# Weight buffers with slack, each weight piece at its own one of sixteen starts 32 bytes apart

## The reference

```python
# block 1 (retention and latent attention)
h = x @ w_in                         # 1024 -> 7744
o = retention(...), causal_attention(rms_norm(mq) @ w_uq, rms_norm(mkv) @ w_ukv)
x = layer_norm(DN_ALPHA * x + concat(gated o) @ w_out)      # 3072 -> 1024
# block 2 (16 heads of attention, gated)
h = x @ w_in                         # 1024 -> 4096
x = layer_norm(DN_ALPHA * x + (merge(o) * silu(g)) @ w_out) # 1024 -> 1024
# block 3 (band attention with 8 heads, a state space mixer, then the feed-forward part)
h = rmsnorm(x) @ w_in_2              # 1024 -> 4112
x = x + concat(attention, ssd) @ w_out_2                    # 1536 -> 1024
x = x + relu(rmsnorm(x) @ w_ff1_2) ** 2 @ w_ff2_2           # 1024 -> 4096 -> 1024
out = rmsnorm(x)
```

## Time and profile before

| | before |
|---|---|
| runs, us | 795.87, 791.13 (median 793.5) |
| profiled execution, span, us | 790.2 |
| its own time | between the runs and the span nothing more is listed; the span is 0.9 us under the faster run |
| PE busy, share of the span | 775.5 us, 98% |
| weight loads (PEld) | 680.4 us, 86% |
| VectorE, ScalarE, GpSimd busy | 65%, 52%, 12% |
| DMA, share of 16 engines' span, hardware and software queue | 52.1%, 1.8% |
| granted TensorE clock | 0.999 of full speed (2.4 GHz) |

### The profile page before, as it was taken

One profiled execution on the slowest core, in us unless ns is written; L12 is line 12 of the kernel. 1 busy time (PEld: TensorE's weight loads), 2 busy tenths in 40 slices (PEclk: granted clock), 3 DMA queues, 4 the chain that ended last, 5 costly groups with the idle time before them and its releaser, 6 DMA issues.

```text
span 790.2 us, 13096 instructions
## 1 busy us (share of the span) xinstructions
PE 775.5 (98%) x5084; PEld 680.4 (86%) x5084; DVE 512.6 (65%) x816; ACT 414.6 (52%) x623; POOL 95.4 (12%) x69
## 2 busy tenths in 40 slices
PE   9999999999999999999999899999999999999997
PEld 8998877799978887999787799889777999999996
DVE  6965656666664658468866874877756755555554
ACT  5534445453664453445765667465655544445443
POOL 2332000000100003111400207500000000000002
PEclk9999999999999999999999999999999999999999
DMA  9855653344664644676832564634217576556541
GB/s 337 320 182 191 203 171 106 120 150 123 200 229 160 185 150 145 209 227 185 260 88 98 164 199 130 206 110 158 86 65 223 188 220 208 176 197 203 174 157 53
DMA packets 77051, 137.43 MB, mean 174 GB/s; under 512 B 7104, under 2 KB 15552, under 8 KB 76992
## 3 DMA queue, kind: packets, MB, share of 16 engines
q1 hardware_dynamic: 75744, 132.15, 52.1%
q0 software_dynamic: 1248, 4.46, 1.8%
HBM read 132.80 MB, written 1.05 MB: 169 GB/s over the span
## 4 chain that ended last, share of the span: by engine, by line
PE 90%; DVE 4%; issue 2%; POOL 2%; ACT 1%; POOLq 0%; ACTq 0%; DVEq 0%
PE acc L1051 13%; PE acc L1053 13%; PE acc L1052 13%; PE acc L1059 13%; PE acc L1061 12%; PE acc L1060 12%; PE acc L1339 1%; PE acc L1373 1%; DVE w_lo L780 1%; PE acc L1216 1%; PE acc L1323 1%; PE acc L1312 1%; PE acc L1252 1%; PE acc L1208 1%; POOL b_lo L780 1%
## 5 line engine op out<-in xcount | busy, mean ns | idle before, releaser
L780 DVE TENSOR_TENSOR w_lo<-raw,w_hi 128x1024 fp32r<-128x1024 f32 (+1 forms) x224 | 273.5, 1236 | 174.0 <-ACT w_hi L760 91.9
L1059 PE MATMUL acc<-x_hi,w_hi 128*128 128x256 f32 x840 | 236.7, 282 | 0.4 <-DVE x_lo L2201 0.4
L1061 PE MATMUL acc<-x_hi,w_lo 128*128 128x256 f32 x840 | 233.9, 278 | 0.0
L1060 PE MATMUL acc<-x_lo,w_hi 128*128 128x256 f32 x840 | 233.9, 278 | 0.0
L760 ACT ACTIVATE w_hi<-raw 128x1024 fp32r<-128x1024 f32 (+1 forms) x128 | 133.3, 1043 | 131.8 <-PE acc L1061 66.4
L750 ACT ACTIVATE w_hi<-raw 128x1024 fp32r<-128x1024 f32 x109 | 115.9, 1063 | 110.9 <-PE acc L1061 58.6
L1059 PEld LDWEIGHTS acc<-x_hi,w_hi 128*128 128x128 f32 x840 | 157.9, 188 | 3.4 <-issue 2.6
L1060 PEld LDWEIGHTS acc<-x_lo,w_hi 128*128 128x128 f32 x840 | 158.6, 189 | 0.8 <-issue 0.5
L1061 PEld LDWEIGHTS acc<-x_hi,w_lo 128*128 128x128 f32 x840 | 158.2, 188 | 0.0
L1051 PE MATMUL acc<-w_hi,cat_hi 128*128 128x512 f32 x272 | 108.9, 400 | 0.2 <-DVE w_lo L780 0.2
L1053 PE MATMUL acc<-w_hi,cat_lo 128*128 128x512 f32 x272 | 107.0, 393 | 0.0
(11 more groups left out here) (297 smaller groups left out, 910.1 us busy)
## 6 DMA issues: line engine op xcount, KB each, us to landing
raw<-in_w_ff SPq DMA_DIRECT2D x32, 1024.0 KB, 5.3
raw<-in_w_in_even SPq DMA_DIRECT2D x28, 1024.0 KB, 5.0
raw<-in_w_in_odd SPq DMA_DIRECT2D x16, 1024.0 KB, 5.4
raw<-in_w_in SPq DMA_DIRECT2D x16, 1024.0 KB, 5.6
raw<-in_w_out_even SPq DMA_DIRECT2D x12, 1024.0 KB, 5.1
raw<-in_w_out SPq DMA_DIRECT2D x4, 1024.0 KB, 5.0
raw<-in_w_in_even SPq DMA_DIRECT2D x4, 512.0 KB, 6.6
raw<-in_w_ukv_even SPq DMA_DIRECT2D x8, 256.0 KB, 3.2
```

What stands on the lines that cost most here:

```text
L780: ins = eng.tensor_tensor(lo, r, hi.bitcast(F32), ALU.subtract)
L1059: pe.matmul(o, wh[:, k, fs], hi[:, ka, :], start=start and f % 2 == 0, stop=False, skip_group_check=True)
L1060: pe.matmul(o, wh[:, k, fs], lo[:, ka, :], start=False, stop=False, skip_group_check=True)
L1061: ins = pe.matmul(o, wl[:, k, fs], hi[:, ka, :], start=False, stop=stop, skip_group_check=True)
```

## The change

Three things change. The descriptor ring is 8192 bytes. `w_hi` and `w_lo` get 128 floats (512 bytes) of slack behind each half, so each is 18432 bytes and not 16384. And each piece gets a `shift` of 8 * (i // 2 * 5 % 16) floats, where i counts the pieces of its layout: places 0, 160, 320, 480, 128 ... bytes, sixteen of them, multiples of 32 bytes, the same for two pieces in a row. The 192 bytes of gap that stood ahead of `x_hi` now stand ahead of `w_hi`. Worked out as above: `w_hi` starts at 36864, `w_lo` at 55296, `x_hi` at 81920, `b_hi` at 98304, `v_hi` at 131072, `cat_hi` at 175104, all multiples of 512. So the distance of a matmul is now the shift of its piece, and 0 still for `v` and `b`. The list of instructions of every engine stays the same, in the same order, with the same waits; only addresses differ. Counted over the program:

| distance, bytes | 0 | 32 | 64 | 96 | 128 | 160 | 192 | 224 | 256 | 288 | 320 | 352 | 384 | 416 | 448 | 480 |
|---|---|---|---|---|---|---|---|---|---|---|---|---|---|---|---|---|
| 256-column matmuls after, feat and tok | 240 | 96 | 192 | 216 | 192 | 192 | 96 | 192 | 144 | 192 | 192 | 96 | 192 | 144 | 192 | 216 |
| 512-column matmuls after | 192 | 96 | 66 | 72 | 48 | 144 | 96 | 66 | 72 | 96 | 120 | 48 | 96 | 84 | 96 | 108 |

Before, 48 of the 512-column and 48 of the 256-column ones are at distance 0 and all others at 320.

```diff
+SLACK = 128
...
-        w_hi = sb("w_hi", [P, 2, 2048], F32R)
-        w_lo = sb("w_lo", [P, 2, 2048], F32R)
+        sb("w_gap", [P, 48])
+        w_hi = sb("w_hi", [P, 2, 2 * (HALF + SLACK)], F32R)
+        w_lo = sb("w_lo", [P, 2, 2 * (HALF + SLACK)], F32R)
         res = sb("res", [P, T, D])
-        sb("x_gap", [P, 48])
...
+        for layout, apart in (("feat", 2), ("tok", 2)):
+            for i, p in enumerate(q for q in pieces if q.chunk.layout == layout):
+                p.shift = 8 * (i // apart * 5 % 16)
...
+        def place(p, e):
+
+            if p.home in (0, 1):
+                return p.off + e + (p.off + e) // HALF * SLACK + p.shift
+            return p.off + e
+
+        def weights_of(p):
+
+            def tiles(b):
+                return [b[:, place(p, k * p.cols):place(p, k * p.cols) + p.cols] for k in range(p.nk)]
+            return [tiles(b) for b in room_of(p)]
+
         def split_views(p, k0, k1):
...
-            parts = [b[:, p.off + k0 * p.cols:p.off + k1 * p.cols] for b in room_of(p)]
+            at = place(p, k0 * p.cols)
+            parts = [b[:, at:at + (k1 - k0) * p.cols] for b in room_of(p)]
...
-                wh, wl = [b[:, p.off:p.off + p.size].rearrange("p (k n) -> p k n", k=p.nk) for b in room_of(p)]
+                wh, wl = weights_of(p)
...
-                            pe.matmul(o, xh, wh[:, k, :], start=start, stop=False)
+                            pe.matmul(o, xh, wh[k], start=start, stop=False)
...
-    nc = _bacc.Bacc("TRN2", target_bir_lowering=False, num_devices=1)
+    nc = _bacc.Bacc("TRN2", target_bir_lowering=False, num_devices=1, dynamic_dma_scratch_size=8192)
```

More of the change, by code:

```diff
@@ L125, in __init__ @@
         self.off = 0
+        self.shift = 0
         self.home = None
@@ L686, in split_views @@
             if p.order == "beside":
-                both = room_of(p)[0][:, p.off:p.off + 2 * p.size].rearrange("p (k c n) -> p k c n", k=p.nk, c=2)
+                both = room_of(p)[0][:, at:at + 2 * p.size].rearrange("p (k c n) -> p k c n", k=p.nk, c=2)
                 return [(r.rearrange("p (k n) -> p k n", k=p.nk), both[:, :, 0, :], both[:, :, 1, :])]
@@ L1050, in products_of @@
                             xh, xl = hi[:, ka, t * P:(t + 1) * P], lo[:, ka, t * P:(t + 1) * P]
-                            pe.matmul(o, xh, wh[:, k, :], start=start, stop=False)
-                            pe.matmul(o, xh, wl[:, k, :], start=False, stop=False)
-                            ins = pe.matmul(o, xl, wh[:, k, :], start=False, stop=stop or (t == 1 and k == p.nk - 1 and p is down[1].pieces[-2]))
+                            pe.matmul(o, xh, wh[k], start=start, stop=False)
+                            pe.matmul(o, xh, wl[k], start=False, stop=False)
+                            ins = pe.matmul(o, xl, wh[k], start=False, stop=stop or (t == 1 and k == p.nk - 1 and p is down[1].pieces[-2]))
                     else:
@@ L1057, in products_of @@
                             fs = slice(f * P, (f + 1) * P)
-                            pe.matmul(o, wh[:, k, fs], hi[:, ka, :], start=start and f % 2 == 0, stop=False, skip_group_check=True)
-                            pe.matmul(o, wh[:, k, fs], lo[:, ka, :], start=False, stop=False, skip_group_check=True)
-                            ins = pe.matmul(o, wl[:, k, fs], hi[:, ka, :], start=False, stop=stop, skip_group_check=True)
+                            pe.matmul(o, wh[k][:, fs], hi[:, ka, :], start=start and f % 2 == 0, stop=False, skip_group_check=True)
+                            pe.matmul(o, wh[k][:, fs], lo[:, ka, :], start=False, stop=False, skip_group_check=True)
+                            ins = pe.matmul(o, wl[k][:, fs], hi[:, ka, :], start=False, stop=stop, skip_group_check=True)
                     if p.full and k == p.nk // 2 - 1:
@@ L1082, in products_of_tokens @@
                     xh, xl = hi[:, ka, t * P:(t + 1) * P], lo[:, ka, t * P:(t + 1) * P]
-                    pe.matmul(o, xh, wh[:, k, :], start=start, stop=False)
-                    pe.matmul(o, xh, wl[:, k, :], start=False, stop=False)
-                    ins = pe.matmul(o, xl, wh[:, k, :], start=False, stop=stop)
+                    pe.matmul(o, xh, wh[k], start=start, stop=False)
+                    pe.matmul(o, xh, wl[k], start=False, stop=False)
+                    ins = pe.matmul(o, xl, wh[k], start=False, stop=stop)
                     if t and k == 1:
@@ L1102, in last_columns @@
                     xh, xl = hi[:, ka, P:2 * P], lo[:, ka, P:2 * P]
-                    pe.matmul(o, xh, wh[:, k, cs], start=k == 0, stop=False)
-                    pe.matmul(o, xh, wl[:, k, cs], start=False, stop=False)
-                    ins = pe.matmul(o, xl, wh[:, k, cs], start=False, stop=k == p.nk - 1)
+                    pe.matmul(o, xh, wh[k][:, cs], start=k == 0, stop=False)
+                    pe.matmul(o, xh, wl[k][:, cs], start=False, stop=False)
+                    ins = pe.matmul(o, xl, wh[k][:, cs], start=False, stop=k == p.nk - 1)
                 own(ins, "piece_used" if h else "tokens_used")
@@ L1124, in rows_of @@
                                 k = 4 * h + j
-                                ins = pe.matmul(acc[32 * j:32 * j + 32, c.pair, 0, ts], w_hi[:, p.home, p.off + 32 * k:p.off + 32 * k + 32].bitcast(F32), x[:, k, ts].bitcast(F32),
+                                ins = pe.matmul(acc[32 * j:32 * j + 32, c.pair, 0, ts], w_hi[:, p.home, place(p, 0) + 32 * k:place(p, 0) + 32 * k + 32].bitcast(F32), x[:, k, ts].bitcast(F32),
                                                 start=(h == 0 and x is hi), stop=(h > 0 and x is lo), skip_group_check=True)
                 else:
-                    wh, wl = [b[:, p.off:p.off + p.size].rearrange("p (k n) -> p k n", k=p.nk) for b in room_of(p)]
+                    wh, wl = weights_of(p)
                     o = acc[:, c.pair, t, 0:p.cols]
@@ L1134, in rows_of @@
                         start, stop = p is c.pieces[0] and k == 0, p is c.pieces[-1] and k == p.nk - 1
-                        pe.matmul(o, hi[:, p.k0 + k, ts], wh[:, k, :], start=start, stop=False)
-                        pe.matmul(o, hi[:, p.k0 + k, ts], wl[:, k, :], start=False, stop=False)
-                        ins = pe.matmul(o, lo[:, p.k0 + k, ts], wh[:, k, :], start=False, stop=stop)
+                        pe.matmul(o, hi[:, p.k0 + k, ts], wh[k], start=start, stop=False)
+                        pe.matmul(o, hi[:, p.k0 + k, ts], wl[k], start=False, stop=False)
+                        ins = pe.matmul(o, lo[:, p.k0 + k, ts], wh[k], start=False, stop=stop)
                 if t:
```

## The result

The changed kernel took 801.94 and 802.47 us, median 802.2, against 793.5 before: ratio 1.0115, 95% interval 1.0086 to 1.0144. It is 8.7 us slower, by an interval that lies clear of 1. Its profiled execution has a span of 800.1 us, 9.9 over the 790.2 of before.

What follows compares the result with a forecast made beforehand. PE was taken as the bound, with time the number of float32r matmuls times their spacing. Terms +6.2 - 1.9 + 0.6 = +4.9 us on the 793.5 median gave 798.4 us, predicted as 798, range 785 to 809.

Steps and rivals of the forecast that it cites:

- 256 columns, +6.2 us forecast: 256-column float32r matmuls on PE: mean spacing 117.7 ns over 2760 matmuls, +6.2 us, bounds -6.0 and +12.5.
- 512 columns, -1.9 us forecast: 512-column float32r matmuls on PE: mean spacing 227.8 ns over 1500 matmuls, -1.9 us, bounds -4.0 and +6.4.
- Settling, +0.6 us: Stretches on PE: each added change of distance costs some 15 ns while the spacing settles, 39 times, +0.6 us.
- Slack, ring, ScalarE, VectorE, order: nothing: Buffer slack, 8 KB descriptor ring, ScalarE and VectorE writes, and instruction order: each costs nothing or is hidden by waits.
- Rival 1: PE spacing: places don't matter, entry into each stretch sets the rate; 793.5 us, give or take 2.4; chance 0.26.
- Rival 2: PE stretches: changing distance frees PE from a slow rate; 783.5 us in full, 788.5 for half; chance 0.17.
- Rival 3: Matmuls with pieces at odd multiples of 32 bytes: each pays a full step, 13.9 us on top, 812.3 us; chance 0.11.
- Rival 4: 512-column matmuls: some distances have no conflict; about 767 us at all places but 0, 4 us at a quarter; chance 0.04.
- the estimate of about 20 us: 512-column matmuls: if the skill page's 215.8 ns held at all other distances, the sum would be about 20 us lower.
- The reason for the lower bound at 256 columns: 256-column matmuls on PE: spacing can't be closer than the weight load, 111.9 ns, so 113.3 is all but the floor.

Runs made afterwards that it cites:

- the finer map: The changed kernel with its sixteen places set 16 bytes apart over 256 bytes, not 32 bytes apart; 803.45 us.
- the three mixtures: The changed kernel with one shift for all pieces (320, 320, 0 bytes) and w_lo 192, 64, 64 bytes further on than w_hi; 805.24, 802.39 and 801.44 us.

## Why the prediction was right, and where it was not

The bound, the direction and the range were right: PE is the bound, no other engine or queue moved by more than tenths of a us, and the time is count times spacing, with the spacing set by the distance. The size was 8.7 us, not 4.9, because one of two terms had the wrong sign.

- **256 columns, +6.2 us forecast, 6.6 measured.** The mean of the two distances seen, 117.7 ns, is what sixteen distances give, 117.9, and the bounds 113.3 and 120.0 held as means of a distance in the changed kernel (single spacings go to 125, and the finer map has one place at 120.9). That the number came out is partly luck: the two seen happened to lie near the two ends of the map, 115.4 and 120.0, so their mean fell in its middle. The reasoning is the same that failed for 512 columns.
- **512 columns, -1.9 us forecast, 4.4 measured.** This is the term that failed, taken "in the same way", from "nothing makes an unseen one nearer to either": 227.8 ns was forecast, 232.2 measured. The trace before showed 0 and 320, and by the map these are the two good ones of the eight that differ modulo 256 (228 to 231); the six unseen ones have 232 to 234, about the upper bound of 233.3 that I had from the earlier trace rows and up to 0.8 over it. Taking the mean of what is seen is only fair if the seen ones are a sample. These were not; the layout before stood at good places.
- **Settling, +0.6 us**, was too small to be told apart.
- **Slack, ring, ScalarE, VectorE, order: nothing.** Slack, ring and addresses together cost 0.8 us at 320 bytes and 0 at 64 by the medians (at most 2.1 by the narrower interval), the ring alone nothing. ScalarE and VectorE kept their lengths.
- **Rival 1, places don't matter:** refuted by one distance for all at 0 (801.8) against 64 (793.2). Its other half, the entry sets the rate, is true at 64 and 320 for both shapes, and the changed kernel's two stretches at 448 show it there too. It does not hold at 0 and 32: those kernels have four runs each within 0.5 us (0.9 with both operands at 32), those at 64 and 320 ten each within 4.6 and 6.0. The rule of the Trainium skill that I set beside it, "SBUF — State Buffer", section "Who interferes with whom", has PE's two read ports independent. The runs here do not agree for these matmuls: with nothing moved but one operand against the other, 512 columns take 226.7 or 233.3 ns.
- **Rival 2, moving on frees PE from a slow rate:** at 320 the changed kernel did run at 113.3 in all its 190 spacings of 256 columns, but at 64 at 117.8, and the other distances cost more than this could give.
- **Rival 3, the odd places:** as a price of a start off a multiple of 64 it is refuted by both operands at 32 bytes. That odd places are slow for 512 columns (232.7 to 234.1) is true as a distance. At no place was the price a full step on top of the even ones.
- **Rival 4, distances without conflict:** none among sixteen, nor at the eight places between. The Trainium skill, "TensorE: Matmul & The Clock Gate", section "Back-to-back issue gap", gives 215.8 ns for 512 columns, and gives it for a single matmul by itself; it was reached nowhere, the lowest settled spacing is 226.7. Two sums were off there: beside 226.4 the gain to 215 is 11.4 ns and not 12.8, so this rival gave 14.9 us and about 769; and the estimate of about 20 us fits all 1500 matmuls, while the 1188 at unseen distances give 14.
- **The reason for the lower bound at 256 columns** was wrong: I took the 111.9 ns of the load for it. With half the columns to load the spacing still is 113.3. What holds it there is not shown; the figure is 17 cycles for 16 columns, as it is with 512.

What stays open is the mechanism below the distances: why 17 for 16, why the pattern repeats after 256 bytes, and what in an entry picks 113.3 or 117.8. That the load of the next matmul is the one that meets the stream fits the places at which the rate changes, but no kernel was made to test it.

## What to carry to other kernels

In a kernel that TensorE bounds with float32r matmuls, read the spacing of starts by stretch before anything else: it is not one number, and the distance of weight to activation operand modulo 256 bytes was worth up to 6% of it for 256 columns and 3% for 512, 1.4% of this kernel's time (804.3 against 793.2 us). Choose one distance for the whole kernel by measurement (here 64; 0 is best for 512 columns alone, but using both won nothing) and give hi and lo buffers the same one, since the three mixtures tried all took over 801 us. Spreading buffers over many places takes the average of the map, which is worse than where a layout already stands well. And when unseen cases are priced by the mean of the seen ones, ask whether the seen ones were chosen.

## What was not expected of the hardware

- The spacing of back-to-back float32r matmuls goes with the difference of their two operands' SBUF addresses (weight less activation) modulo 256 bytes: 113.3 to 120.9 ns for 256 columns, 226.7 to 234.2 for 512; a common shift of both by 32 changes nothing (226.7 at 0/0 and at 32/32, 233.3 at 32/0).
- At distance 64 (and 320) two rates are stable, 113.3 and 117.8 ns for 256 columns, 228.9 and 233.3 for 512. A rate holds to the end of a stretch, for tens of us. By an estimate this makes up nearly all of the 6 us over which the runs of one program spread (790.3 to 796.8 in 25 runs); at 0 or 32 four runs each agree within 0.5 us.
- Half as many stationary columns, and so a shorter weight load, make 256-column matmuls faster (120.0 to 113.3 ns) and 512-column ones slower (226.7 to 230).
- 17 cycles of 2.4 GHz for 16 columns (113.3 and 226.7 ns) is the lowest settled spacing in all fourteen kernels, for both shapes.
